# Gathering an expert's rows feature-major: the one-hot as the moving operand

## What is computed

```
logits = x2 @ w_router + b_router
top_v, top_i = lax.top_k(logits, 4);  gate = softmax(top_v)
for each expert e, over the tokens x that chose it:
    hb  = x @ w_gate_up[e] + b_gate_up[e]            # (., 2048)
    glu = min(hb[:, :1024], 7);  lin = clip(hb[:, 1024:], -7, 7)
    act = glu * sigmoid(1.702 * glu) * (lin + 1)
    y   = act @ w_down[e] + b_down[e]
    out[token] += gate * y
```

## Time and profile before

| what | value |
|---|---|
| three runs | 1539.68 us median (1532.11 to 1541.16) |
| the profiled execution | 1537.03 us |
| its span | 1535.2 us |
| mean granted PE clock | 0.974 |
| PE busy | 1431.1 us (93%) |
| DMA, the queue of the loads | 479.91 MB |
| PE, old gather L1047 | 384 records, 98.5 us |
| PE, turn_x L1055 | 128 records, 21.9 us |
| ACT, xg copy L1411 | 32, 18.7 us |

### The profile page before, as it was taken

One profiled execution on the slowest core, in us unless ns is written; L12 is line 12 of the kernel. 1 busy time (PEld: TensorE's weight loads), 2 busy tenths in 40 slices (PEclk: granted clock), 3 DMA queues, 4 the chain that ended last, 5 costly groups with the idle time before them and its releaser, 6 DMA issues.

```text
span 1535.2 us, 17760 instructions
## 1 busy us (share of the span) xinstructions
PE 1431.1 (93%) x7309; PEld 689.8 (45%) x7309; DVE 507.6 (33%) x1113; ACT 244.9 (16%) x450; POOL 141.5 (9%) x120
## 2 busy tenths in 40 slices
PE   6998997999999989999999999999999999999996
PEld 5776996548787532333333233323332333233321
DVE  3677533231301223542242223223322322232225
ACT  4332243002210200111011011101110110010012
POOL 0144011010000001000100010001000100100010
PEclk9999999999999868999999999999999999999998
DMA  5513145943546828999999999999999999999991
GB/s 201 216 61 83 56 127 165 296 154 124 176 153 258 351 105 364 417 418 418 415 417 418 417 415 417 418 416 415 418 418 416 416 418 417 415 418 417 418 412 69
DMA packets 128856, 481.40 MB, mean 314 GB/s; under 512 B 16683, under 2 KB 35243, under 8 KB 95707
## 3 DMA queue, kind: packets, MB, share of 16 engines
q1 hardware_dynamic: 128678, 479.91, 79.0%
q0 software_dynamic: 96, 0.33, 0.1%
HBM read 469.15 MB, written 11.26 MB: 313 GB/s over the span
## 4 chain that ended last, share of the span: by engine, by line
PE 44%; DMA 41%; SPq 5%; issue 4%; DVE 3%; ACT 1%; POOL 0%; DVEq 0%; POOLq 0%; ACTq 0%
DMA gus<-in_w_gate_up 38%; PE bank L1069 11%; PE bank L620 5%; PE bank L1088 4%; SPq L500 4%; PE bank L989 4%; PE bank L859 3%; PE bank L599 3%; PE bank L1047 2%; PE bank L608 2%; PE bank L1005 2%; PE bank L1113 2%; DMA Ssg<-in_state_gdn 1%; DVE Ssg L1833 1%; SPq L438 1%
## 5 line engine op out<-in xcount | busy, mean ns | idle before, releaser
L1069 PE MATMUL bank<-gus,xT 128*64 128x512 f32 x2048 | 460.8, 596 | 39.7 <-DMA gus<-in_w_gate_up 37.4
L1069 PEld LDWEIGHTS bank<-gus,xT 128*64 128x64 f32 x2048 | 139.9, 137 | 354.8 <-issue 239.1
L2076 DVE TENSOR_TENSOR glu<-bank,bgb 128x512 f32<-128x512 f32 x32 | 22.1, 691 | 655.7 <-issue 398.0
L1088 PE MATMUL bank<-dns,acT 128*64 128x512 f32 x1024 | 228.5, 599 | 0.0
L1565 POOL PARTITION_BROADCAST bgb<-bgu x32 | 41.7, 1302 | 1053.3 <-DMA bgu<-in_b_gate_up 858.1
L1088 PEld LDWEIGHTS bank<-dns,acT 128*64 128x64 f32 x1024 | 71.0, 138 | 136.2 <-issue 136.2
L2099 DVE TENSOR_TENSOR X<-X,bank 128x512 f32<-128x512 f32 (+1 forms) x198 | 121.0, 673 | 18.2 <-PE bank L1113 13.1
L620 PE MATMUL bank<-HT,wslot 128*128 128x264 f32 x512 | 119.3, 388 | 0.0
L620 PEld LDWEIGHTS bank<-HT,wslot 128*128 128x128 f32 x512 | 95.3, 190 | 19.6 <-issue 4.6
L1047 PE MATMUL bank<-hrow,O 128*64 128x512 f32 (+1 forms) x384 | 98.5, 632 | 3.3 <-DVE O L2059 3.3
L1113 PE MATMUL bank<-yb,CT 64*128 64x512 f32 (+1 forms) x384 | 94.5, 607 | 2.0 <-ACT CT L1431 1.6
(11 more groups left out here) (372 smaller groups left out, 1166.8 us busy)
## 6 DMA issues: line engine op xcount, KB each, us to landing
gus<-in_w_gate_up SPq DMA_DIRECT2D x256, 1024.0 KB, 20.5
dns<-in_w_down SPq DMA_DIRECT2D x128, 1024.0 KB, 22.0
wslot<-in_w_in SPq DMA_DIRECT2D x18, 2048.0 KB, 8.3
out<-Ssg SPq DMA_DIRECT2D x8, 512.0 KB, 5.4
Ssr<-in_state_ret SPq DMA_DIRECT2D x4, 1024.0 KB, 13.6
out<-Ssr SPq DMA_DIRECT2D x4, 1024.0 KB, 8.0
wslot<-in_w_branch_b SPq DMA_DIRECT2D x2, 2048.0 KB, 7.8
wslot<-in_w_branch_a SPq DMA_DIRECT2D x2, 2048.0 KB, 7.7
```

What stands on the lines that cost most here:

```text
L1069: t = pe.matmul(B[part][64 * g:64 * g + 64, :], block_of(xT, k), gus[k][:, D * part + 512 * g:D * part + 512 * g + 512], start=(k == 0), s ...
L1088: t = pe.matmul(B[2][64 * g:64 * g + 64, :], block_of(acT, k), dns[4 * u + k // 2][:, k % 2, 512 * g:512 * g + 512], start=(k == 0), stop= ...
```

## The change

The gather's two operands change places. The stationary operand is now a block of hrow, r tokens by 128 features, and the moving one is the one-hot O with 64 slots. Per expert there are 8 feature blocks times 3 token tiles, 24 products of 64 columns. Each writes [128 features, 64 slots] to its place in B[4], in the layout that turn_x had produced, so x_out copies it to xT as before. B[3], xg, rows_out and turn_x are not used for this any more; semaphores m_gx and m_gxev go, and onehot waits on m_tx in place of m_gx.

```
@@ PE
+            def gather(b):
+                after(pe, m_O, 1, b, 1)
+                after(pe, m_txev, 1, b)
+                for k in range(KT):
+                    for c, r in TILES:
+                        t = pe.matmul(block_of(B[4], k), hrow[0:r, c, P * k:P * k + P], O[0:r, c, :],
+                                      start=(c == 0), stop=(c == 2))
+                t.then_inc(m_tx, 1)
-            def gather(b):
-                after(pe, m_O, 1, b, 1)
-                after(pe, m_gxev, 1, b)
-                for c, r in TILES:
-                    for g in range(2):
-                        t = pe.matmul(B[3][64 * g:64 * g + 64, :], O[0:r, c, :], hrow[0:r, c, 512 * g:512 * g + 512],
-                                      start=(c == 0), stop=(c == 2))
-                t.then_inc(m_gx, 1)
-            def turn_x(b):
-                after(pe, m_gxev, 1, b, 1)
-                after(pe, m_txev, 1, b)
-                for j in range(4):
-                    t = pe.transpose(B[4][:, P * j:P * j + P], xg[:, P * j:P * j + P], ident)
-                t.then_inc(m_tx, 1)
@@ PE, combine and biases
-                        after(pe, m_gxev, 1, gathered, 1)
-                        pe.wait_ge(m_gxev, 3)
@@ PE, order
             gather(0)
-            turn_x(0)
 ...
             gather(1)
             gate_up(0)
-            turn_x(1)
 ...
                     biases()
-                if b + 1 < NE:
-                    turn_x(b + 1)
                 down(b - 1, (b - 1) % 2, 16 * ((b - 1) // 2) + 16)
@@ ACT
-            def rows_out(b):
-                after(act, m_gx, 1, b, 1)
-                after(act, m_tx, 1, b)
-                nc.scalar.copy(xg[:, :], B[3][:, :]).then_inc(m_gxev, 1)
@@ DVE, onehot
-                after(dve, m_gx, 1, b)
+                after(dve, m_tx, 1, b)
```

More of the change, by code:

```diff
@@ L230, in build_layer @@
         CT = mnew("CT", [P, TOK])
-        xg, glu, lin, xT = [mnew(n, [P, 512]) for n in ("xg", "glu", "lin", "xT")]
+        glu, lin, xT = [mnew(n, [P, 512]) for n in ("glu", "lin", "xT")]
         bgb = mnew("bgb", [P, 2, 512])
@@ L352, in build_layer @@
         m_wd = [sem(f"m_wd{k}") for k in range(KT)]
-        (m_bgu, m_bb, m_O, m_Ow, m_gx, m_gxev, m_tx, m_txev, m_guc, m_gu, m_b1, m_b2, m_glu, m_lin, m_lin2, m_sig,
+        (m_bgu, m_bb, m_O, m_Ow, m_tx, m_txev, m_guc, m_gu, m_b1, m_b2, m_glu, m_lin, m_lin2, m_sig,
          m_act, m_ta, m_taev, m_dc, m_d, m_yev, m_tc, m_tcev, m_cb, m_acc) = [sem(n) for n in (
-             "m_bgu", "m_bb", "m_O", "m_Ow", "m_gx", "m_gxev", "m_tx", "m_txev", "m_guc", "m_gu", "m_b1", "m_b2",
+             "m_bgu", "m_bb", "m_O", "m_Ow", "m_tx", "m_txev", "m_guc", "m_gu", "m_b1", "m_b2",
              "m_glu", "m_lin", "m_lin2", "m_sig", "m_act", "m_ta", "m_taev", "m_dc", "m_d", "m_yev", "m_tc", "m_tcev",
@@ L1101, in _, with combine @@
             homes = ((B[6], B[7]), (B[5], B[3]), (B[0], B[1]))
-            def combine(b, turned, gathered, activated):
+            def combine(b, turned, activated):
                 after(pe, m_tcev, 1, b, 1)
@@ L1149, in _ @@
                 if b >= 2:
-                    combine(b - 2, b - 1, min(b + 1, NE - 1), b)
+                    combine(b - 2, b - 1, b)
                 else:
                     biases()
-                if b + 1 < NE:
-                    turn_x(b + 1)
                 down(b - 1, (b - 1) % 2, 16 * ((b - 1) // 2) + 16)
@@ L1158, in _ @@
             turn_c(NE - 2)
-            combine(NE - 2, NE - 1, NE - 1, NE - 1)
+            combine(NE - 2, NE - 1, NE - 1)
             down(NE - 1, 1, 16 * (NE // 2))
@@ L1162, in _ @@
             turn_c(NE - 1)
-            combine(NE - 1, NE - 1, NE - 1, NE - 1)
+            combine(NE - 1, NE - 1, NE - 1)
             def extra(j, b):
@@ L1167, in extra @@
                 gather(b)
-                turn_x(b)
                 gate_up(b)
@@ L1172, in extra @@
                 down(b, 0, j * 16 + (16 * (NE // 2) + 16))
-                combine(b, b, b, b)
+                combine(b, b, b)
             extra_blocks(pe, extra)
@@ L1436, in y_out @@
                 nc.scalar.copy(yb[:, :], B[2][:, :]).then_inc(m_yev, 1)
-            rows_out(0)
             x_out(0)
@@ L1441, in _ @@
             nc.scalar.copy(ZT[:, :], B[6][0:NE, 0:TOK]).then_inc(s_ztev, 1)
-            rows_out(1)
             sigmoid(0)
@@ L1450, in _ @@
                 if b + 1 < NE:
-                    rows_out(b + 1)
                     x_out(b + 1)
@@ L1459, in extra @@
             def extra(j, b):
-                rows_out(b)
                 x_out(b)
```

## The result

The changed kernel takes 1755.39 us in the median of four runs (1753.74 to 1759.2), the kernel before 1539.58 us: a ratio of 1.1413, with a 95% interval from 1.1383 to 1.1443. That is slower by 14%, 215.8 us. The forecast was 1780 us.

What follows compares the result with a forecast made beforehand. PE was taken to bound the expert stage early, the weights' DMA late. With 37.4 us of PE per expert, the stage adds 218 us and the start 25: 243 on 1537.0 gives 1780 us; 8-in-10 range 1607 to 1825.

Steps and rivals of the forecast that it cites:

- The bound changes sides: Expert stage: PE becomes the bound throughout, 32.3 us per expert at full clock against 30.4 of DMA.
- The load sets the pace: New gather: 48 records at 0.1115 us each, 5.35 us at full clock; a shorter stream buys nothing.
- The last rival, hidden loads: Gather: loads hide behind the stream, 2.7 us at full clock, DMA keeps the bound, 1535 us; chance 0.07.
- the point of 5.8 us: Gather length at full clock below which the DMA keeps the bound and above which PE paces all.
- Changes of rows: New gather: 16 steps into or out of the 8-row tile at 0.15 us each, 2.4 us, gather 7.75 us.
- The case without step costs: Gather: neither steps nor clock cost, 5.35 us at full clock, 29.9 us per expert, 1551 us; chance 0.10.
- The clock: Falls from 2.4 to 1.2 GHz in each gather until some 3 us into down, costing 5.1 us per expert; chance 0.63.
- The case in which the clock holds: Expert stage: no clock falls in the gathers, 32.3 us per expert, 1626 us; chance 0.20.
- The start: First gathers, at half clock, take 12.7 us each; gate_up(2) comes 25 us late.

Runs made afterwards that it cites:

- the run without changes: Changed kernel with the third token tile filled with zeros to 128 rows, so no load changes its number of rows: 1558.07 us, ratio 1.0123.
- the four pieces: Changed kernel with the gather cut into four pieces around combine and within down, DVE's next one-hot moved behind the sums: 1638.71 us, ratio 1.0647.
- the first version with four pieces: Changed kernel with the gather cut into the same four pieces, DVE's next one-hot still ahead of the sums: 1740.3 us, ratio 1.132.

## Why the prediction was right

The mechanism held in its parts, and their sizes were off by little.

- *The bound changes sides.* PE paces the stage for the whole of it: 300 us busy in 300 from 1000 to 1300 us, where the kernel before had 283.75, and memory at 339 GB/s (forecast "near 340").
- *The load sets the pace.* Forecast 5.35 us for 48; measured 5.50 with the one change before them, and the same with half the stream. The last rival, hidden loads, is out. The Trainium skill, "TensorE: Matmul & The Clock Gate", "Back-to-back issue gap", says that in a stream of loads and products both set the spacing, and that its formula by columns, meant for products without loads, counts too little when few are streamed. The traces agree: 0.11 us per record with 32, 64 or 128 columns. A kernel with 5.5 us of gather indeed lands in the reach of before, as the point of 5.8 us in that rival said.
- *Changes of rows.* Forecast 0.15 each, measured 0.14. The gather is 7.58 us at full clock, forecast 7.75. The case without step costs is out, since the run without changes has a gather 2.08 us shorter than that.
- *The clock.* Forecast to fall in each gather and to return some 3 us into down. It does fall in each, for instance from 1028.3 to 1038.4 us, but it returns there only 0.2 us into down. It is low for 9.3 us per expert in the mean and costs 36.4 - (28.05 - 3.46 + 7.58) = 4.2 us; I had 10.2 and 5.1, taken from the one low stretch that before had shown. This is the term that was mis-sized: 29 times 0.9 is 26 us. The shorter gather (29 x 0.17 = 5 us) goes the same way, and the later first gather (3.55 us) the other, which together is the distance between 1780 and the 1754.19 us of the profiled execution. The case in which the clock holds, 1626 us, is what the four pieces gave when it was kept, 1639 us with their cuts. The Trainium skill's rule that ties a fall to pauses of PE ("TensorE: Matmul & The Clock Gate", "Why this matters for your kernels") does not cover the changed kernel: there was no pause. Where PE does pause, in the first version with four pieces, a fall followed 14 of 29 pauses. What in thin work brings the clock down, the few columns or the few rows or the gaps at the changes, is separated here only for the columns.
- *The start.* Forecast 25 us, measured 25.4; each gather 13.3 us at the low clock, forecast 12.7.

Of the 216 us, by the runs: 117 are the clock, changed kernel against the four pieces. Their cuts cost some 9 us of their own, so the clock's part lies somewhat higher; 29 x 4.2 from the trace is 122. From the four pieces to all 128 rows are 81: the changes of rows with 29 x 2.08 = 60, those cuts, and 12 at the start. The remaining 18 are loads: some 13 at the start, where 48 take 10.5 us, and some 6 in the 29 experts of 30.09 us. What the change takes away, 3.46 us per expert, was less than half of what the 24 new products need even at full clock, and in the late half PE had 2.3 us to spare.

## What to carry to other kernels

When the operands of a product change places, count loads of stationary columns, not multiplications: 128 columns of f32 cost 0.11 us a record at full clock, two records a product, with 32, 64 or 128 columns streamed. Keep short tiles together or fill them with zeros: a change of the rows in use costs 0.14 us, and the gather with zeros, which has none inside, took 5.50 us in place of 7.58. And look at the granted clock of neighbouring pieces that were not touched: combine at 5.52 for 2.88 us told the story here.

## What had not been expected

- Less work made the kernel slower by 100 us: with 32 streamed columns in place of 64 and everything else in the gather equal, the clock fell, and the time went from 1558 to 1658 us. More work made it faster by 197 us: zeros in 120 rows of the array.
- The same gather in four pieces between dense products kept the clock at 1.00, while in two halves it was lost in 23 experts and kept in 6, in one and the same run.
- Halving the number of changes gave 61 us, where their own price gives 29 x 8 x 0.14 = 32 at full clock. The experts lost 29 x 1.8 = 52 us, the other 20 by a shorter time at the low clock; 5 us went at the start, and 4 lie ahead of the first gather, where the two kernels don't differ.
